# Two layers of routed experts: from whole tiles of one expert to pairs of half tiles, each expert's weights brought from HBM once

## The chip, the cores and the metric

The program runs on one core of a Trainium2 chip (cores 0 to 7; here core 0 alone). The metric is the device time of one execution in microseconds. Runs of this kernel agree within about 0.5%.

## What is computed

The program computes a first transformer block, then two more blocks whose feed-forward part is a mixture of experts. The change touches only these two mixtures. In `second_block`, layer 0 sends 768 tokens (512 and 256 of a context) and layer 1 sends 512 tokens through `hier_moe`:

```python
def hier_moe(h, wg, bg, we, be, w_gate, w_up, w_down):
    g_idx = jnp.argmax(g_logits, axis=-1)                      # 4 groups of 4 experts
    e_sel = jnp.take_along_axis(e_logits, g_idx[:, None, None], axis=1)[:, 0]
    top_p, top_i = lax.top_k(jax.nn.softmax(e_sel, axis=-1), MOE_TOPK)   # 2 experts per token
    ...
    for g in range(MOE_GROUPS):
        a = jnp.einsum('nd,edf->nef', h, w_gate[g])            # 1024 -> 256
        u = jnp.einsum('nd,edf->nef', h, w_up[g])
        hid = jax.nn.silu(a) * u * combine[:, g, :, None]
        out = out + jnp.einsum('nef,efd->nd', hid, w_down[g])  # 256 -> 1024
    return out
```

There are 16 experts of 3 MB each (gate, up and down, 1 MB each, all in float32). Every token goes to two of them, so layer 0 has 1536 rows to compute and layer 1 has 1024. With the given inputs the reference routes this many rows to experts 0 to 15:

```
layer 0: 79 97 97 109 94 105 102 115 86 73 75 72 132 95 107 98
layer 1: 69 77 83 89 37 35 36 36 86 70 62 72 60 77 71 64
```

## The kernel before

The kernel is a list of stages. In a stage the engines work side by side; at its end they all meet (`meet`, L2495). For a mixture the stages are a norm, `Router` (scores, choice of experts, and the normed tokens stored to HBM as `moe_rows`), `Dispatch`, `Experts` and `Combine` (L2428 to L2436).

`Dispatch` (L1710) works out on VectorE where each row goes. Every expert's rows are laid out in tiles of 128 rows, and a tile belongs to one expert. The program can't know how full experts will be, so it always computes the most tiles that could be needed: `tiles_bound` (L1705) gives 27 for layer 0 and 23 for layer 1. With the counts above 17 and 16 of them hold rows; the others are computed all the same, with expert 15. `row_token` says which token stands in which row, `tile_expert` which expert each tile has.

`Experts` (L1844) handles one tile per step, and all its engines run the same software pipeline. In the step of tile t:

- POOL gathers the 128 token rows of a coming tile from HBM (512 KB, L2014).
- TensorE (L1906) multiplies tile t by gate and up (8 products of 128x128 by 128x512, L1917; the profile counts two instructions for each float32 product), transposes the rows of tile t+1 (8, L1889), multiplies tile t-1 by down (4 products, L1902), and transposes the hidden values of tile t (2, L1927).
- ScalarE takes half of each result out of PSUM and issues the DMA that stores a tile's result as `moe_out` (512 KB, L1957). VectorE takes the other half.

Weights come through `ring`, six slots of 1 MB in SBUF shared by all stages. SyncE issues all weight loads in program order (`Ring.fill`, L239). A slot is loaded again when the counter `weights_used` says that TensorE is done with it. For experts `ExpertLoads` (L1796) reads `tile_expert` into a register and loads three slots per tile: two with gate and up for half of the 1024 inputs each (four DMAs of 512 KB in rows of 1 KB, L1830) and one with down (1 MB in rows of 4 KB, L1832). It starts when the lists are ready (L1836). Two tiles' weights fit in the ring. The order of work is given by the program text of each engine and by semaphores; nothing reorders it.

```python
            for c in range(DK):
                g = w.slot(p, c // 4).rearrange("p (c n) -> p c n", c=4)
                last = pe.matmul(ps[:, p, :], mo.xT[:, p, c, :], g[:, c % 4, :], start=(c == 0), stop=(c == DK - 1))
```

## Time and profile before

| | us |
|---|---|
| three runs | 2707.84, 2712.48, 2719.38 (median 2712.48) |
| profiled execution | 2714.23 |
| its span | 2712.4 |
| experts of layer 0, first gather to last down product | about 1571.7 to 1928.0 |
| experts of layer 1, the same | about 2373.7 to 2677.6 |

Times in the trace are counted from the start of the span. "PE" is TensorE, "PEld" its weight loads, "SPq" and "ACTq" the instructions by which SyncE and ScalarE issue DMAs. The DMA share is how much of the time the core's 16 DMA engines had a packet in work. "PEclk" is the granted TensorE clock as a share of 2.4 GHz.

### The profile page before, as it was taken

The numbers are of one execution on the slowest core, as the hardware profiler recorded it, in microseconds if no ns is written. First come the engines' busy times: TensorE is split into PE (matmuls) and PEld (weight loads), VectorE is DVE, ScalarE is ACT, GpSimd is POOL, SyncE is SP. The second block draws the span as 40 slices with busy tenths as digits, with TensorE's granted clock in tenths as the row PEclk, the third lists the DMA queues.
The fourth block names the chain that finished last, engine by engine and source line by source line (L and its number), as shares of the span: only waits on it lengthen the run. The fifth ranks groups of instructions, "written<-read, shape, count | busy, mean of one in ns | idle before, by whom it ended". The sixth has DMA issues, their size and how long they took to land. (4 is left out here: it accounts for less than half of the span.)

```text
span 2712.4 us, 27356 instructions
## 1 busy us (share of the span) xinstructions
PE 2316.3 (85%) x10248; PEld 1270.3 (47%) x10248; DVE 769.3 (28%) x1768; ACT 540.0 (20%) x1153; POOL 151.4 (6%) x159
## 2 busy tenths in 40 slices
PE   5999999899999969997789579999467889579994
PEld 2456554444444435644664534444143665434442
DVE  1012551100010035863532411111237552411112
ACT  1013441100010023221530311111121441211111
POOL 3000000000000001200000000000100000000001
PEclk9997999999999989998999679999788899689997
DMA  7236873112122120010100179999710000199996
GB/s 248 71 93 231 296 282 111 47 62 93 62 86 70 56 97 32 32 62 1 48 17 0 64 261 317 331 334 332 250 65 31 1 1 1 41 307 337 330 335 208
DMA packets 212457, 382.69 MB, mean 141 GB/s; under 512 B 10935, under 2 KB 147351, under 8 KB 206208
## 3 DMA queue, kind: packets, MB, share of 16 engines
q1 hardware_dynamic: 185792, 285.57, 32.5%
q0 software_dynamic: 17312, 62.08, 6.5%
q10 hardware_dynamic: 9248, 33.59, 3.0%
q8 instruction: 73, 1.20, 0.2%
q14 instruction: 32, 0.26, 0.0%
HBM read 344.42 MB, written 42.02 MB: 142 GB/s over the span
## 5 line engine op out<-in xcount | busy, mean ns | idle before, releaser
L1917 PE MATMUL ps<-ring,T 128*128 128x512 f32 x800 | 363.6, 608 | 33.8 <-DMA ring<-in_exp_w_up 25.5
L283 PE MATMUL ps<-ring,HT 128*128 128x512 f32 (+1 forms) x832 | 350.4, 582 | 7.3 <-ACTq L2497 4.3
L2108 PE MATMUL ps<-ring,HT 128*128 128x512 f32 x704 | 304.8, 593 | 3.4 <-issue 2.6
L1917 PEld LDWEIGHTS ps<-ring,T 128*128 128x128 f32 x800 | 150.8, 194 | 217.2 <-issue 217.2
L283 PEld LDWEIGHTS ps<-ring,HT 128*128 128x128 f32 x832 | 158.1, 191 | 197.9 <-issue 188.0
L2108 PEld LDWEIGHTS ps<-ring,HT 128*128 128x128 f32 x704 | 132.9, 190 | 174.7 <-issue 173.7
L1902 PE MATMUL ps<-ring,Z 128*128 128x512 f32 x400 | 180.1, 593 | 1.0 <-ACT Z L1972 1.0
L593 ACT ACTIVATE T<-T,nm 128x128 f32<-128x128 f32 (+5 forms) x208 | 139.8, 673 | 190.8 <-DVE nm L657 190.8
L365 PE MATMUL ps<-ident,T 128*128 128x128 f32 x240 | 39.6, 345 | 141.6 <-DVE T L354 141.6
L547 PE MATMUL ps<-ident,T 128*128 128x128 f32 x752 | 116.4, 288 | 44.4 <-DVE T L315 25.8
L283 PE MATMUL ps<-ring,T 128*128 128x512 f32 x352 | 151.6, 593 | 0.8 <-ACTq L2497 0.7
L1266 PE MATMUL ps<-ring,HT 128*128 128x512 f32 (+1 forms) x384 | 149.2, 545 | 0.5 <-issue 0.5
L2001 DVE TENSOR_TENSOR Z<-ps,Z 128x256 f32<-128x256 f32 x50 | 21.3, 426 | 410.3 <-ACT Z L1965 410.3
L547 PEld LDWEIGHTS ps<-ident,T 128*128 128x128 f32 x752 | 82.0, 143 | 102.3 <-ACT T L593 57.3
L529 PE MATMUL ps<-T 64*128 64x256 f32 (+1 forms) x960 | 118.1, 372 | 10.5 <-DVE nm L657 8.4
L564 PE MATMUL ps<-T,Z 128*64 128x128 f32 x1504 | 111.1, 291 | 0.3 <-DVE T L315 0.3
L1902 PEld LDWEIGHTS ps<-ring,Z 128*128 128x128 f32 x400 | 72.2, 190 | 74.1 <-issue 74.1
L283 PEld LDWEIGHTS ps<-ring,T 128*128 128x128 f32 x352 | 66.7, 190 | 85.1 <-issue 84.2
L365 PEld LDWEIGHTS ps<-ident,T 128*128 128x128 f32 x240 | 38.3, 185 | 145.6 <-issue 145.6
L1266 PEld LDWEIGHTS ps<-ring,HT 128*128 128x128 f32 x384 | 72.0, 191 | 69.4 <-issue 66.0
L2128 DVE TENSOR_TENSOR Z<-ps,T 128x256 f32<-128x256 f32 x44 | 18.7, 425 | 290.1 <-ACT T L2120 290.1
L529 PEld LDWEIGHTS ps<-T 64*128 64x128 f32 x960 | 82.1, 194 | 37.3 <-issue 17.4
(309 smaller groups left out, 2276.0 us busy)
## 6 DMA issues: line engine op xcount, KB each, us to landing
ring<-in_exp_w_gate SPq DMA_DIRECT2D x100, 512.0 KB, 8.0
ring<-in_exp_w_up SPq DMA_DIRECT2D x100, 512.0 KB, 9.1
ring<-in_exp_w_down SPq DMA_DIRECT2D x50, 1024.0 KB, 6.1
ring<-in_mod_w SPq DMA_DIRECT2D x48, 1024.0 KB, 4.8
moe_out<-Z ACTq DMA_DIRECT2D x50, 512.0 KB, 6.6
ring<-in_w_gate SPq DMA_DIRECT2D x22, 512.0 KB, 3.7
ring<-in_w_up SPq DMA_DIRECT2D x22, 512.0 KB, 4.8
ring<-in_w_in SPq DMA_DIRECT2D x10, 1024.0 KB, 15.6
```

Source lines behind the costliest of these rows:

```text
L283: last = pe.matmul(self.banks.bank(u0 + i)[0:self.rows, 0:cn], self.lhs(k0 + c, t), w[:, c, :], start=(k0 + c == 0), stop=(k0 + c == self. ...
L365: last = pe.transpose(self.banks.bank(u)[:, j * P:(j + 1) * P], k.HN[:, t, c * P:(c + 1) * P], k.ident[:, :])
L529: last = pe.matmul(s, u["q"](h), kT(h)[:, done:done + m], start=True, stop=True)
L547: last = pe.transpose(self.t.bank(c)[:, b * P:(b + 1) * P], src, k.ident[:, :])
L564: last = pe.matmul(k.ps[64 * h:64 * h + 64, 7, ui * P:(ui + 1) * P], v(h), self.PT[:, j % 2, h, b * P:(b + 1) * P], start=(b == 0), stop=( ...
L593: act.activation(p, p, ACT.Exp, scale=-1.0, bias=k.nm[:, pi % 2, c:c + 1], accum_out=k.den[:, pi % 2, c:c + 1]).then_inc(k.probs_done.sem, 1)
L1266: last = pe.matmul(self.lin.bank(u)[:, 0:cn], k.HT[:, c, t * P:(t + 1) * P], w[:, c % 4, :], start=(c == 0), stop=(c == DK - 1))
L1902: last = pe.matmul(ps[:, 5 + hf, :], mo.hidT[:, p, c, :], wd[:, c, hf * 512:(hf + 1) * 512], start=(c == 0), stop=(c == 1))
L1917: last = pe.matmul(ps[:, p, :], mo.xT[:, p, c, :], g[:, c % 4, :], start=(c == 0), stop=(c == DK - 1))
L2001: dve.tensor_tensor(mo.hid[:, p, :], ps[:, p, EXH:2 * EXH], mo.silu[:, p, :], ALU.mult).then_inc(self.hid_ready[0], 1)
L2108: last = pe.matmul(self.gu.bank(i), k.HT[:, c, t * P:(t + 1) * P], w[:, c % 4, :], start=(c == 0), stop=(c == DK - 1))
L2128: self.gu.take(i, dve.tensor_tensor(k.Zb(FFN)[:, t, j * EXH:(j + 1) * EXH], self.gu.bank(i)[:, EXH:2 * EXH], k.silub[:, i % 2, :], ALU.mult))
```

## The change

Rows are laid out in half tiles of 64 rows, each of one expert (every expert has at least one). Two neighbouring halves make a pair, which is what a step handles. `pairs_bound` gives 20 pairs for layer 0 and 16 for layer 1. With the counts above, 33 and 25 halves hold rows; the rest, up to 40 and 32, are computed with expert 15.

A product over 128 rows becomes two over 64: the first half's rows go to PSUM partitions 0 to 63, the second half's to 64 to 127, each with its own weights. The expert's weights lie in one of three "places" of 3 MB (the ring's six slots and half of `HT`, now one tensor `wide`). The first half reads its weights from the place. For the second half ScalarE issues two DMAs per pair, which copy the weights within SBUF from the place of that half's expert to fixed buffers: `wgu` (2 MB, gate and up) and `wd` (1 MB, down), two of each.

SyncE now loads each of the 16 experts once per layer, in order, from a new input `experts`, which the host lays out so that each DMA moves 1 MB in rows of 8 KB per partition. Experts 0 and 1 are loaded as soon as the ring's slots are free (before the norm), expert 2 when the router is done with `HT`, and expert e+3 when the last pair of expert e is done (`last_pair`, worked out in `Dispatch`). TensorE and ScalarE read `half_expert` into registers in every step. The loops of `Experts` are written out. The buffers `xg`, `xT` move in SBUF. Only when `Experts` ends may the next stage's weights enter the ring.

```diff
@@ constants
+PLACES = 3
+HALF = 64
@@ Router.tensor
+        pe.drain().then_inc(k.places_free.sem, 1)
@@ bound
-def tiles_bound(tokens):
-    return (2 * tokens - NEXP) // P + NEXP
+def pairs_bound(tokens):
+    return ((2 * tokens - NEXP) // HALF + NEXP + 1) // 2
@@ Dispatch.vector, end
+        do(dve.tensor_scalar(mo.last, mo.end, 0.5, -0.5, ALU.mult, ALU.add))
+        count_of(mo.count, mo.last, NEXP, m - 1, ALU.is_ge)
+        dve.tensor_copy(k.last_pair[:, :], mo.count)
@@ ExpertLoads
...
+        k = self.k
+        sp.wait_ge(k.weights_used, self.n0)
+        for e in range(NEXP):
+            a = e % PLACES
+            if e == PLACES - 1:
+                sp.wait_ge(k.places_free.sem, self.freed + 1)
+            if e == PLACES:
+                sp.wait_ge(k.lists_ready.sem, self.lists + 1)
+            if e >= PLACES:
+                last = sp.value_load(k.last_pair[0:1, e - PLACES:e - PLACES + 1], min_val=0, max_val=63)
+                sp.wait_ge(k.pairs_done.sem, last + (self.done + 1))
+            for j in range(2):
+                sp.dma_start(k.places[:, a, j, :], self.w[e, j]).then_inc(k.gu_landed[a].sem, 16)
+            if e:
+                self.announce_down(sp, e - 1)
+            sp.wait_ge(k.gu_landed[a].sem, self.gu_landed[a] + 32 * (e // PLACES + 1))
+            sp.drain().then_inc(k.experts_ready.sem, 1)
+            if e >= PLACES:
+                sp.wait_ge(k.pairs_done.sem, last + (self.done + 2))
+            sp.dma_start(k.places[:, a, 2, :], self.w[e, 2]).then_inc(k.down_landed[a].sem, 16)
+        self.announce_down(sp, NEXP - 1)
+    def announce_down(self, sp, e):
+        k, a = self.k, e % PLACES
+        sp.wait_ge(k.down_landed[a].sem, self.down_landed[a] + 16 * (e // PLACES + 1))
+        sp.drain().then_inc(k.experts_ready.sem, 1)
+    def expert_of(self, eng, half):
+        return eng.value_load(self.k.half_expert[0:1, half:half + 1], min_val=0, max_val=NEXP - 1)
+    def await_gate_up(self, eng, e):
+        eng.wait_ge(self.k.experts_ready.sem, 2 * e + (self.ready + 1))
+    def await_down(self, eng, e):
+        eng.wait_ge(self.k.experts_ready.sem, 2 * e + (self.ready + 2))
+    def slots(self, e, j0, j1):
+        return self.k.places[:, bass.ds(e % PLACES, 1), j0:j1, :].rearrange("p o j n -> p (o j) n")
+    def columns(self, e, j, c0, n=512):
+        return self.k.places[:, bass.ds(e % PLACES, 1), j, c0:c0 + n].rearrange("p o n -> p (o n)")
@@ Experts.tensor
+        def down(t, e):
+            p = t % 2
+            self.after(pe, self.down_copied[p], 16 * (t // 2 + 1))
             self.after(pe, self.hid_out, t + 1)
-            if not (isinstance(t, int) and t == 0):
+            if t:
                 self.after(pe, self.y_out_act, t)
                 self.after(pe, self.y_out_dve, t)
-            wd = w.slot(p, 2).rearrange("p (c n) -> p c n", c=2)
             for hf in range(2):
                 for c in range(2):
-                    last = pe.matmul(ps[:, 5 + hf, :], mo.hidT[:, p, c, :], wd[:, c, hf * 512:(hf + 1) * 512],
+                    at = 1024 * c + 512 * hf
+                    pe.matmul(ps[low, 5 + hf, :], mo.hidT[:, p, c, low], w.columns(e, 2, at), start=(c == 0), stop=(c == 1))
+                    last = pe.matmul(ps[high, 5 + hf, :], mo.hidT[:, p, c, high], mo.wd[:, p, at:at + 512],
                                      start=(c == 0), stop=(c == 1))
             last.then_inc(self.y_full[0], 1)
-        def step(b, p, final):
-            t = 2 * b + p
-            peeled = isinstance(t, int)
-            w.landed(pe, b, p, 0)
-            w.landed(pe, b, p, 1)
+        x_transposes(0)
+        e = w.expert_of(pe, 0)
+        before = None
+        for t in range(m):
+            p = t % 2
+            self.after(pe, self.gu_copied[p], 16 * (t // 2 + 1))
             self.after(pe, self.x_out_act, t + 1)
             self.after(pe, self.x_out_dve, t + 1)
-            if not (peeled and t < 2):
+            if t >= 2:
                 self.after(pe, self.hid_ready, t - 1)
             for c in range(DK):
-                g = w.slot(p, c // 4).rearrange("p (c n) -> p c n", c=4)
-                last = pe.matmul(ps[:, p, :], mo.xT[:, p, c, :], g[:, c % 4, :], start=(c == 0), stop=(c == DK - 1))
+                j, at = c // 4, 512 * (c % 4)
+                pe.matmul(ps[low, p, :], mo.xT[:, p, c, low], w.columns(e, j, at), start=(c == 0), stop=(c == DK - 1))
+                last = pe.matmul(ps[high, p, :], mo.xT[:, p, c, high], mo.wgu[:, p, j, at:at + 512],
+                                 start=(c == 0), stop=(c == DK - 1))
             last.then_inc(self.gu_full[0], 1)
-            if not final:
-                x_transposes(b + (p == 1), 1 - p)
-            first = peeled and t == 0
-            if not first:
-                down(b - (p == 0), 1 - p)
-            pe.drain().then_inc(k.weights_used, 2 if first else 3)
+            if t + 1 < m:
+                x_transposes(t + 1)
+            if t:
+                down(t - 1, before)
+            pe.drain().then_inc(k.pairs_done.sem, 1)
+            before = e
+            if t + 1 < m:
+                e = w.expert_of(pe, 2 * t + 2)
             self.after(pe, self.hid_ready, t + 1)
             for c in range(2):
                 last = pe.transpose(ps[:, 4 + 3 * p, c * P:(c + 1) * P], mo.hid[:, p, c * P:(c + 1) * P], k.ident[:, :])
             last.then_inc(self.hid_transposed[0], 1)
-        def epilogue(b, p):
-            down(b - (p == 0), 1 - p)
-            pe.drain().then_inc(k.weights_used, 1)
-        self.run(pe, lambda: x_transposes(0, 0), step, epilogue)
+        down(m - 1, before)
+        pe.drain().then_inc(k.pairs_done.sem, 1)
+        pe.drain().then_inc(k.weights_used, SLOTS)
@@ Experts.scalar
+        def gate_up_copy(t):
+            second[t] = w.expert_of(act, 2 * t + 1)
+            if t >= 2:
+                self.after(act, self.gu_full, t - 1)
+            w.await_gate_up(act, second[t])
+            act.dma_start(mo.wgu[:, t % 2, :, :], w.slots(second[t], 0, 2)).then_inc(self.gu_copied[t % 2][0], 16)
+        def down_copy(t):
+            if t >= 2:
+                self.after(act, self.y_full, t - 1)
+            w.await_down(act, second[t])
+            act.dma_start(mo.wd[:, t % 2, :].unsqueeze(1), w.slots(second[t], 2, 3)).then_inc(self.down_copied[t % 2][0], 16)
         def step(b, p, final):
             t = 2 * b + p
             peeled = isinstance(t, int)
+            if not final:
+                gate_up_copy(t + 1)
             self.after(act, self.gu_full, t + 1)
             if not (peeled and t < 2):
                 self.after(act, self.hid_ready, t - 1)
...
             act.activation(mo.hidT[:, p].rearrange("p c n -> p (c n)"), ps[:, 4 + 3 * p, 0:EXH], ACT.Copy).then_inc(self.hid_out[0], 1)
             if not first:
                 y_store(b - (p == 0), 1 - p)
+            down_copy(t)
@@ buffers
+        wide = sb("wide", [P, SLOTS * SLOT + DK * NT * P])
+        k.ring = wide[:, 0:SLOTS * SLOT].rearrange("p (s n) -> p s n", s=SLOTS)
+        k.HT = wide[:, SLOTS * SLOT:SLOTS * SLOT + DK * NT * P].rearrange("p (c n) -> p c n", c=DK)
+        k.places = wide[:, 0:PLACES * 3 * SLOT].rearrange("p (a j n) -> p a j n", a=PLACES, j=3)
+        mo.wd = k.Z[:, at[0]:at[0] + 2 * SLOT].rearrange("p (a n) -> p a n", a=2)
+        mo.wgu = T[:, 0:4 * SLOT].rearrange("p (a j n) -> p a j n", a=2, j=2)
@@ lay_out
+    gate, up = (np.asarray(inputs[n]).reshape(2, NEXP, 2, 4, P, EXH) for n in ("exp_w_gate_2", "exp_w_up_2"))
+    down = np.asarray(inputs["exp_w_down_2"]).reshape(2, NEXP, 1, 2, P, D)
+    both = np.stack([gate, up], 5).transpose(0, 1, 2, 4, 3, 5, 6).reshape(2, NEXP, 2, P, SLOT)
+    a["experts"] = np.ascontiguousarray(np.concatenate([both, down.transpose(0, 1, 2, 4, 3, 5).reshape(2, NEXP, 1, P, SLOT)], 2))
```

The step in the order of the engines. First TensorE, in the middle of a tile's step before (`ps` is PSUM, `Z` and `T` are SBUF buffers):

```order
L1917 MATMUL ps<-ring,T 128x512 x8
L1889 MATMUL ps<-ident,T 128x128 x8
L1902 MATMUL ps<-ring,Z 128x512 x4
L1927 MATMUL ps<-ident,Z 128x128 x2
```

and from the down products of a pair's step to the first gate and up products of the next, now:

```order
L1923 ISA
L1923 MATMUL ps<-wide,Z 64x512
L1924 MATMUL ps<-Z 64x512
L1851 TENSOR_LOAD half_expert
L1851 ISA x2
L1954 MATMUL ps<-ident,Z 128x128 x2
L1940 ISA
L1940 MATMUL ps<-wide,Z 64x512
L1941 MATMUL ps<-T,Z 64x512
```

Each product is now two of half the width, the first with an address worked out in a register (`ISA`); after the down products TensorE's sequencer reads the next pair's expert.

ScalarE, one step before and one now:

```order
L1965 ACTIVATE Z<-ps 128x256 [waits moe_hid_ready,moe_gu_full]
L1945 ACTIVATE T<-ps 128x512 [waits moe_x_transposed]
L1950 ACTIVATE Z<-ps 128x512 [waits y_stored_0,moe_y_full]
L1972 ACTIVATE Z<-ps 128x256 [waits moe_hid_transposed]
L1957 DMA moe_out<-Z 128x1024 [waits moe_y_out_dve,moe_y_out_act]
```

```order
L1992 ISA [waits experts_ready]
L1992 DMA T<-wide 128x4096
L2008 ACTIVATE Z<-ps 128x256 [waits moe_hid_ready,moe_gu_full]
L1970 ACTIVATE Z<-ps 128x512 [waits moe_x_transposed]
L1975 ACTIVATE Z<-ps 128x512 [waits y_stored_1,moe_y_full]
L2015 ACTIVATE Z<-ps 128x256 [waits moe_hid_transposed]
L1982 DMA moe_out<-Z 128x1024 [waits moe_y_out_dve,moe_y_out_act]
L1857 REGISTER_ALU [waits moe_y_full]
L1998 ISA [waits experts_ready]
L1998 DMA Z<-wide 128x2048
```

The copy of gate and up for the next pair stands ahead of the step's first activation, the copy of down for this pair behind its last; both wait for SyncE's word that the expert has landed.

SyncE, the loads at the start of layer 1 and of the first expert that needs a used place, now:

```order
L1835 DMA wide<-in_experts 128x2048 [waits weights_used]
L1835 DMA wide<-in_experts 128x2048
L1842 DMA wide<-in_experts 128x2048 [waits gate_up_landed_0]
L1835 DMA wide<-in_experts 128x2048 x2
L1842 DMA wide<-in_experts 128x2048 [waits down_landed_0,gate_up_landed_1]
L1835 DMA wide<-in_experts 128x2048 [waits places_free]
L1835 DMA wide<-in_experts 128x2048
L1842 DMA wide<-in_experts 128x2048 [waits down_landed_1,gate_up_landed_2]
L1832 TENSOR_LOAD last_pair [waits lists_ready]
```

Three experts' loads now stand ahead of the wait for the lists; all loads stood behind it.

## Rows read from the trace of the kernel before

**Rows 1.** The page: busy time; then busy, clock and DMA tenths in 40 slices.

```profile
PE 2316.3 (85%) x10248; PEld 1270.3 (47%) x10248; DVE 769.3 (28%) x1768; ACT 540.0 (20%) x1153; POOL 151.4 (6%) x159
...
PEclk9997999999999989998999679999788899689997
DMA  7236873112122120010100179999710000199996
```

**Rows 2.** Windows: start:end, length, busy us of engines, PEclk, DMA share, GB/s.

```profile
1494.00:1567.00 73.00, 36.80 (x203) 34.43 (x202) 35.74 (x151) 20.90 (x37) 2.65 (x5) 0.61 0.16 60
1595.00:1919.00 324.00, 304.41 (x865) 141.18 (x866) 44.22 (x75) 46.81 (x101) 22.19 (x24) 0.99 0.99 323
2396.00:2669.00 273.00, 256.31 (x729) 118.86 (x728) 36.30 (x63) 39.17 (x84) 17.92 (x19) 0.99 0.97 321
...
260.00:330.00 70.00, 68.33 (x690) 41.10 (x688) 37.16 (x126) 33.17 (x100) 5.55 (x9) 1.00 0.83 303
```

**Rows 3.** Timeline of TensorE, layer 0: start, length, line, work [idle before <-releaser].

```profile
1583.52 9.87 PE L1917 MATMUL ps<-ring,T 128*128 128x512 f32 x16 [0.94 <-DVE T L1988]
...
1595.15 7.11 PE L1917 MATMUL ps<-ring,T 128*128 128x512 f32 x16 [0.35 <-DVE T L1988]
1602.09 1.04 PE L1889 MATMUL ps<-ident,T 128*128 128x128 f32 x8
1602.97 3.60 PE L1902 MATMUL ps<-ring,Z 128*128 128x512 f32 x8
1606.67 0.43 PE L1927 MATMUL ps<-ident,Z 128*128 128x128 f32 x2
1607.09 7.10 PE L1917 MATMUL ps<-ring,T 128*128 128x512 f32 x16
...
1619.96 0.67 PE L1917 MATMUL ps<-ring,T 128*128 128x512 f32 x1 [0.92 <-issue]
```

**Rows 4.** The page's groups and the waits of 1570 to 1920 us: DMA's part.

```profile
L1917 PE MATMUL ps<-ring,T 128*128 128x512 f32 x800 | 363.6, 608 | 33.8 <-DMA ring<-in_exp_w_up 25.5
...
PE ps L1917 <- DMA ring<-in_exp_w_up: 15.4, 19, 3.0
```

**Rows 5.** DMA queues: packets, MB, share of 16 engines; issues: count, KB each, us to landing.

```profile
DMA packets 212457, 382.69 MB, mean 141 GB/s; under 512 B 10935, under 2 KB 147351, under 8 KB 206208
...
q1 hardware_dynamic: 185792, 285.57, 32.5%
q0 software_dynamic: 17312, 62.08, 6.5%
q10 hardware_dynamic: 9248, 33.59, 3.0%
...
ring<-in_exp_w_down SPq DMA_DIRECT2D x50, 1024.0 KB, 6.1
ring<-in_mod_w SPq DMA_DIRECT2D x48, 1024.0 KB, 4.8
moe_out<-Z ACTq DMA_DIRECT2D x50, 512.0 KB, 6.6
```

**Rows 6.** Timelines: first gather (POOL) and last down products (PE) of both layers.

```profile
1571.71 1.03 POOL L2014 DMA_INDIRECT T<-moe_rows,row_token  x1 [53.84 <-DVEq L2497]
2373.70 0.99 POOL L2014 DMA_INDIRECT T<-moe_rows,row_token  x1 [38.60 <-DVEq L2497]
...
1924.33 3.67 PE L1902 MATMUL ps<-ring,Z 128*128 128x512 f32 x8 [0.52 <-ACT Z L1972]
2673.92 3.67 PE L1902 MATMUL ps<-ring,Z 128*128 128x512 f32 x8 [0.52 <-ACT Z L1972]
```

**Rows 7.** Timelines of TensorE in attention: products onto 64 columns of the array.

```profile
299.31 1.07 PE L558 MATMUL ps<-T,vcmp 31*64 31x512 f32 x4
...
1302.35 1.53 PE L564 MATMUL ps<-T,Z 128*64 128x128 f32 x24
1303.81 0.49 PE L529 MATMUL ps<-T 64*128 64x256 f32 x2
```

**Rows 8.** SyncE's reads of `tile_expert`: ns min/median/max.

```profile
L1820 SPq TENSOR_LOAD <-tile_expert x50: 262/268/485, 1568.1 to 2649.7; - x50
```

**Rows 9.** Timeline of VectorE in `Dispatch`: two of its small steps.

```profile
1556.65 0.21 DVE L1765 TENSOR_SCALAR Z<-Z 128x96 f32<-128x96 f32 x1
1556.90 0.26 DVE L1766 TENSOR_TENSOR Z<-Z 128x96 f32<-128x96 f32 x1
```

More of the change, by code:

```diff
@@ L1767, in vector @@
-        do(dve.tensor_tensor(tile, whole, over_tokens(mo.first), ALU.add))
-        do(dve.tensor_scalar(tmp, whole, -float(P), None, ALU.mult))
-        do(dve.tensor_tensor(rank, rank, tmp, ALU.add))
-        for i in range(2):
-            for x, to in ((tile, mo.at_tile), (rank, mo.at_row)):
-                do(dve.tensor_tensor(tmp, mo.chosen[:, i, 0:n, :], x, ALU.mult))
-                do(dve.tensor_reduce(to[:, i, 0:n], tmp, AXX, ALU.add))
+        do(dve.tensor_scalar(mo.count, mo.count, 1.0 / HALF, None, ALU.mult))
@@ L1835, in fill, with __init__ @@
-    def fill(self, sp):
-        sp.wait_ge(self.k.lists_ready.sem, self.ready + 1)
-        with sp.Fori(0, self.m // 2) as b:
-            self.load(sp, b, 0)
-            self.load(sp, b, 1)
-        if self.m % 2:
-            self.load(sp, self.m // 2, 0)
+    def __init__(self, k, l, A, router, dispatch):
+        self.k, self.w = k, A["experts"][l]
+        self.n0 = k.rg.lend(self)
+        self.freed, self.lists = router.freed, dispatch.ready
+        uses = [len(range(a, NEXP, PLACES)) for a in range(PLACES)]
+        self.gu_landed = [t.reserve(32 * n) for t, n in zip(k.gu_landed, uses)]
+        self.down_landed = [t.reserve(16 * n) for t, n in zip(k.down_landed, uses)]
+        self.ready = k.experts_ready.reserve(2 * NEXP)
+        self.done = k.pairs_done.reserve(dispatch.m + 1)
@@ L1980, in epilogue @@
                 act.wait_ge(self.y_stored[q][0], self.y_stored[q][1] + 16 * ((self.m + 1 - q) // 2))
-        self.run(act, lambda: x_out(0, 0), step, epilogue)
+        self.run(act, first, step, epilogue)
     def vector(self, dve, ch):
```

158 lines of the change are left out of this document (72 added, 86 removed).

## The prediction

> **What bounds the kernel now.** I read the page first, to see where the change can act. TensorE is busy 85% of the span, and the DMA tenths stand at 9 in two stretches only [rows 1]: these are the two `Experts` stages, and they are all that the change is about. The windows over them show DMA shares of 0.99 and 0.97 at 323 and 321 GB/s, and a TensorE clock of 0.99 [rows 2]. So 16 DMA engines have no room left. The timeline of TensorE then shows that it has hardly any either: a step without a wait lasts from 1595.15 to 1607.09, 11.94 us [rows 3], and 27 steps of that are 322 us of the 356.3 us from the first gather (1571.7) to the last down product (1928.0) [rows 6]. The waits agree: TensorE waits for gate and up 15.4 us in layer 0 and 25.5 us in both layers [rows 4]. The two limits are within 6% of each other, so cutting one alone gives little. Layer 1 takes 303.9 us (2373.7 to 2677.6) [rows 6].
>
> **The products.** 50 steps become 36. Each has the same transposes and twice as many products of half the width. Whether that costs a whole step or two is read in attention, where products onto 64 columns of the array alternate between its halves: four instructions of 512 columns take 1.07 us, and 24 of 128 columns 1.53 us [rows 7]. A full-width instruction of 512 costs 0.43 us (8 in 3.60) and one of 128 about 0.11 (8 in 1.04, the last one's tail of 0.16 in it) [rows 3]. One after the other they would take 1.9 and 2.8 us; side by side 1.02 and 1.5. So the halves run side by side, and a pair costs what a tile costs, 11.94 us. Changing between 128 and 64 columns shows no gap at 1303.81 [rows 7]. The new read of `half_expert` stands behind the down products and before the hidden transposes. It costs at least nothing, since the sequencer may be ahead; its load alone is 0.27 us on SyncE [rows 8], and the nearest row for a sequencer that holds up products is the 0.92 us at a loop's start [rows 3]. I take 0.9, as it stands right behind a drain: 12.8 us a step. 36 steps are 461 us; TensorE is then not what ends a stage, if the bytes don't follow.
>
> **The bytes.** They don't. A tile moves 3 MB of weights, 0.5 MB gathered and 0.5 MB stored, 4.19 MB by the issues [rows 5]. A pair moves the same gather and store, 3.15 MB of copies within SBUF, and, while experts are still being loaded, 3.15 MB from HBM per expert: 7.34 MB. The copies run on the same engines and take the place of the loads that were saved. I count what must be moved before the step that first needs expert 15, since after it no load is left. Layer 0, pair 15: gate and up copies of 16 pairs 33.6 MB, down copies of 14 pairs 14.7, 13 stores 6.8, 17 gathers 8.9, and 13 experts without the last down 39.8 (three are there before): 103.8 MB. Layer 1, pair 12 (four pairs there use two experts): 27.3 + 11.5 + 5.2 + 7.3 + 39.8 = 91.1 MB.
>
> The rate has to be chosen. Weights now come in rows of 1 KB; loads become rows of 8 KB, copies at least that. The lower bound is today's mix, 323/0.99 = 326 GB/s [rows 2]. The upper bound is ScalarE's queue with packets of 4 KB: 33.59 MB in 3.0% of 16 x 2712.4 us is 25.8 GB/s an engine, 413 GB/s for 16 [rows 5]. Between them lies the stretch in which `mod_w` is loaded, the only packets of 8 KB or more (6249 of them) [rows 5]: 303 GB/s at a share of 0.83, 365 GB/s at a full one [rows 2]. I take that, since its kind is nearest, and a share of 0.97 as in layer 1 now: 354 GB/s. No row shows a copy within SBUF.
>
> Layer 0: 103.8/0.354 = 293.2 us, then five steps that TensorE bounds, four of 12.8 and one with the last down products (12.8 + 0.5 + 3.7 = 17.0): 361.4 us against 356.3, **+5**. Layer 1: 91.1/0.354 = 257.3, three steps of 12.8 and 17.0: 312.7 against 303.9, **+9**.
>
> The Trainium skill has a rule that weighs these bytes otherwise (SBUF — State Buffer, the summary of rules for kernel authors): reckon 358 GB/s between HBM and SBUF and 436 GB/s within SBUF. By it, as an estimate, the copies (87.1 MB) and the rest (107.8 MB) would take 501 us at a full share and 517 at 0.97, where I have 550.
>
> **Waits that are added.** ScalarE now waits at `gate_up_copy` for the next expert ahead of its silu (L2008), so silu, both PSUM copies, VectorE's product and the down products stand behind a late load. The load of expert e+3 is issued when pair e is done, its copy must follow, and the product is three steps later: 11.3 us of the step, then a load and a copy, each at most one step of 7.34 MB (20.7 us) and about 2 us to land (1 MB of `mod_w` lands in 4.8 us [rows 5], its bytes need 2.9). That is 57 us against three steps of 20.7: covered, by 5 us. SyncE waits for a landing before it issues the next down load; ScalarE's queue has work meanwhile. ScalarE's two further issues and one read a step fall on an engine busy 46.8 of 324 us [rows 2].
>
> **Outside.** Experts 0 and 1 load during a norm and the router, where the DMA share is 0.16 [rows 2]: hidden. Expert 2 starts when the router's last store is still out, and ScalarE waits for that store: between 0 and 2.1 MB/0.354 = 6 us a layer; I take 2, **+4** in all, as the store is half gone by then. `Dispatch` loses 12 of 28 small steps ahead of the one-hots (0.21 to 0.26 us [rows 9], -3) and gains two and longer ones behind them (about +1.5): **-3** for both layers. The next stage's weights start no later than now.
>
> **Sum.** +5 + 9 + 4 - 3 = +15 on the profiled execution's 2714.2: 2729. It stood 1.7 above the median of the three runs, so 2728 against 2712.5. A measurement of this kernel can tell about 0.5% (13.6 us) from no change: this is just outside. With 345 or 385 GB/s in place of 365 the bytes cost 582 or 522 us in place of 550: 2699 to 2760 is this case's own range.
>
> **Rivals.**
> - *Large rows and SBUF copies go faster* (faster than before). At the upper bound of 413 GB/s and 0.97, 194.9 MB take 486 us, 64 less: 2664. It decides from 385 GB/s on. For it: the store's packets do run at that rate. Against: full-share `mod_w` doesn't. By the rule of the Trainium skill above it would be 34 us less, 2694. Chance 0.28.
> - *The rate stays at today's 326 GB/s*, set by three queues in competition: 598 us, +47, 2775. Chance 0.06.
> - *TensorE falls to its low clock.* It would be idle some 8 us of each step of 20.7. The clock was 0.61 in the stretch before the stage [rows 2], and the first gate and up products took 9.87 us, not 7.11 [rows 3]. If only the start of each step runs at 1.2 GHz, that is 2.8 us of idle time. If whole steps do, they last 2 x 11.94 + 0.9 = 24.8 us, over 27 load-bound steps +111: 2839. The Trainium skill (TensorE: Matmul & The Clock Gate, HAM oscillation) says that a wait for DMA in each tile makes every tile start at the low clock; the 9.87 us agree, and it gives the first of these cases. Chance of the second 0.06.
> - *A copy within SBUF costs twice its bytes*, if reading and writing there share something: 87.1 MB more are 246 us, and the last steps become 20.7 too, +59: 3033. No row speaks for or against. Chance 0.06.
> - *The halves don't run side by side*, so the change doesn't do what it says: steps of 23.3 us (24 products of 0.86), 36 of them, ending 218 us later: about 2930. Rows 7 speak against it. Chance 0.04.
>
> The forecast has 0.50. Of it 0.22 lies within 0.5% and 0.01 below, 0.27 above. So faster 0.29, same 0.22, slower 0.49. From 2664 to 2839 the range leaves out about 0.1 above and 0.1 below.
>
> **What would show it.** Right: DMA share 0.95 or more until pair 15 (layer 0) and 12 (layer 1), steps of 19 to 22 us there and near 12.8 in the last four or three; TensorE waiting for DMA `T<-wide`; low clock in single slices. Four instructions of 64x512 in about 1.02 us show the halves. Wrong: GB/s over 385 at a full share, or a share well under 0.95 (then the chain of load, copy and product bounds, not the bytes), or load-bound steps in which TensorE is busy throughout.

## The result and the profile after

| | before | after |
|---|---|---|
| median of the runs, us | 2711.18 | 2808.65 (2803.84 to 2814.07) |
| ratio, 95% interval | | 1.0355 [1.0325, 1.0386] |
| span of the profiled execution | 2712.4 | 2811.8 |
| experts of layer 0, first gather to last down product | 356.3 | 384.1 |
| from there to the first gather of layer 1 | 445.7 | 455.1 |
| experts of layer 1 | 303.9 | 363.5 |

Slower was the likelier sign in the forecast, but it had +0.6% and the chip shows +3.5%. The 99.4 us of span are +27.8 in layer 0, +59.6 in layer 1, +9.4 between them, +1.9 before the first gather and +0.6 after layer 1. The profiled execution of the change is the slowest of its four runs, 5.4 us above their median, and a stretch in which the programs do the same, from the end of `Combine` to layer 1's first gather, takes 396 to 404 us in the profiles of the change and its variants. So a difference of a few us between two stages of two profiles shows little by itself.

The page of the changed kernel, the lines that answer to [rows 1], [rows 4] and [rows 5]:

```profile
PE 2218.0 (79%) x10636; PEld 1168.9 (42%) x10636; DVE 744.4 (26%) x1712; ACT 515.8 (18%) x1097; POOL 138.3 (5%) x145
...
PEclk9997999999999999999997688899698897777787
DMA  7237871112122210001003598897410003777885
...
DMA packets 113437, 424.91 MB, mean 151 GB/s; under 512 B 9175, under 2 KB 43191, under 8 KB 85664
...
q10 hardware_dynamic: 17600, 139.50, 12.5%
...
L1940 PE MATMUL ps<-wide,Z 128*64 x576 | 267.9, 620 | 44.9 <-DMA T<-wide 44.1
L1923 PE MATMUL ps<-wide,Z 128*64 x288 | 180.1, 784 | 132.4 <-DMA Z<-wide 132.4
...
T<-wide ACTq DMA_DIRECT2D x36, 2048.0 KB, 10.8
...
Z<-wide ACTq DMA_DIRECT2D x36, 1024.0 KB, 12.8
```

TensorE now waits 132 us for the copies of the down weights (`Z<-wide`) and 44 us for those of gate and up, where it was idle for 33.8 us in all ahead of the gate and up products [rows 4]. The DMA tenths stood at 9 in both stages; now they stand at 7 to 9 in layer 0 and at 7 to 8 in layer 1: the stages are slower and the DMA engines are not full. The windows, as in [rows 2], for the middle of layer 0 and for two parts of layer 1:

```profile
1616.00:1850.00 234.00, 156.81 (x642) 54.41 (x643) 19.90 (x33) 21.76 (x45) 10.34 (x11) 0.82 0.89 346
...
2497.00:2573.00 76.00, 30.06 (x118) 10.29 (x120) 3.24 (x6) 3.50 (x8) 1.89 (x2) 0.69 0.70 260
2573.00:2727.00 154.00, 101.91 (x404) 34.39 (x400) 12.19 (x21) 12.81 (x27) 6.60 (x7) 0.80 0.88 323
```

The stretch at 2497 holds two steps and lasts 76 us, with a DMA share of 0.70. That is not a bound by bytes. In the middle of layer 0, 346 GB/s at a share of 0.89 would be 389 GB/s at a full one.

The starts of the gate and up products give the steps (the step of a pair lasts until the next pair's products start). Layer 0: 12.2, 19.7, then 20.1 to 22.7 for pairs 2 to 12, then 13.5, 20.0, 13.5 and three of 13.0. Layer 1: 10.7, 17.8, 20.8, 23.8, **38.3, 37.4**, 15.0, **38.9**, 15.3, 22.6, 22.3, 25.5, 15.1, 13.0, 13.2.

One load-bound step of layer 0 on TensorE's timeline, as in [rows 3] (rows that only repeat are left out):

```profile
1701.39 0.64 PE L1940 MATMUL ps<-wide,Z 128*64 x1
1701.39 0.64 PE L1941 MATMUL ps<-T,Z 128*64 128x512 f32 x1
1701.86 0.59 PE L1940 MATMUL ps<-wide,Z 128*64 x1
...
1708.40 1.09 PE L1910 MATMUL ps<-ident,Z 128*128 128x128 f32 x8
1715.22 1.11 PE L1923 MATMUL ps<-wide,Z 128*64 x1 [5.73 <-DMA Z<-wide]
...
1716.13 1.06 PE L1923 MATMUL ps<-wide,Z 128*64 x1
...
1720.69 0.59 PE L1923 MATMUL ps<-wide,Z 128*64 x1
...
1722.09 0.43 PE L1954 MATMUL ps<-ident,Z 128*128 128x128 f32 x2 [0.81 <-issue]
1722.49 0.64 PE L1940 MATMUL ps<-wide,Z 128*64 x1
```

Three things stand here. The two halves' products start within 0.01 us of each other and a pair of them starts every 0.43 us: they run side by side. The read of the register costs 0.81 us. And in the middle of the step TensorE waits 5.73 us for the down copy; the down products behind it take 1.06 us at first, 0.59 at the end. The granted clock is 1.00 from 1701.4 to 1709.4 and 0.50 from 1715.2 to 1719.0: the level of 2.4 GHz, then of 1.2 GHz, then of 2.4 GHz again.

ScalarE's and SyncE's issues around that step say why the copy is late:

```profile
1701.52 0.33 ACTq L1982 DMA_DIRECT2D moe_out<-Z  x1
1702.37 0.49 ACTq L1998 DMA_DIRECT2D Z<-wide  x1
1703.68 0.50 ACTq L1992 DMA_DIRECT2D T<-wide  x1
```

```profile
1700.28 0.34 SPq L1842 DMA_DIRECT2D wide<-in_experts  x1
1701.28 0.81 SPq L1835 DMA_DIRECT2D wide<-in_experts  x2
1721.37 0.34 SPq L1842 DMA_DIRECT2D wide<-in_experts  x1
1722.38 0.81 SPq L1835 DMA_DIRECT2D wide<-in_experts  x2
```

Everything of a step, 3 MB of loads, 3 MB of copies and the store, is issued within 3.5 us (the last 2 MB of copies are the next pair's gate and up). The down copy, the one needed first, competes with 3 MB of loads that TensorE needs much later, and lands 12.8 us after its issue. The step's end is what releases the next bundle.

### The profile page after: what moved, and what is told of

Its sections match the earlier page's. It is cut to its first block and busy times, and to the rows that moved or that the text cites. A ratio compares the mean times of both kernels' runs of the same rounds, so it can differ in the third digit from the quotient of the medians.

```text
span 2811.8 us, 27432 instructions
## 1 busy us (share of the span) xinstructions
PE 2218.0 (79%) x10636; PEld 1168.9 (42%) x10636; DVE 744.4 (26%) x1712; ACT 515.8 (18%) x1097; POOL 138.3 (5%) x145
## 3 DMA queue, kind: packets, MB, share of 16 engines
q1 hardware_dynamic: 80416, 228.93, 23.8%
q10 hardware_dynamic: 17600, 139.50, 12.5%
## 5 line engine op out<-in xcount | busy, mean ns | idle before, releaser
L291 PE MATMUL ps<-wide 128*128 128x512 f32 (+1 forms) x832 | 349.5, 581 | 7.5 <-ACTq L2556 4.3
L2156 PE MATMUL ps<-wide 128*128 128x512 f32 x704 | 304.8, 593 | 3.4 <-issue 2.6
L1940 PE MATMUL ps<-wide,Z 128*64 x576 | 267.9, 620 | 44.9 <-DMA T<-wide 44.1
L1923 PE MATMUL ps<-wide,Z 128*64 x288 | 180.1, 784 | 132.4 <-DMA Z<-wide 132.4
L1941 PE MATMUL ps<-T,Z 128*64 128x512 f32 x576 | 268.0, 620 | 0.0
L291 PEld LDWEIGHTS ps<-wide 128*128 128x128 f32 x832 | 157.7, 191 | 197.4 <-issue 187.5
L2156 PEld LDWEIGHTS ps<-wide 128*128 128x128 f32 x704 | 132.9, 190 | 174.8 <-issue 173.7
L1924 PE MATMUL ps<-Z 128*64 128x512 f32 x288 | 180.2, 784 | 0.0
L1940 PEld LDWEIGHTS ps<-wide,Z 128*64 128x64 f32 x576 | 79.0, 143 | 205.2 <-issue 205.2
L291 PE MATMUL ps<-wide,T 128*128 128x512 f32 x352 | 151.6, 593 | 0.8 <-ACTq L2556 0.7
L1274 PE MATMUL ps<-wide 128*128 128x512 f32 (+1 forms) x384 | 149.2, 545 | 0.5 <-issue 0.5
L1923 PEld LDWEIGHTS ps<-wide,Z 128*64 128x64 f32 x288 | 48.2, 180 | 237.6 <-issue 237.6
L2049 DVE TENSOR_TENSOR Z<-ps,Z 128x256 f32<-128x256 f32 x36 | 15.3, 425 | 433.7 <-ACT Z L2008 433.7
L291 PEld LDWEIGHTS ps<-wide,T 128*128 128x128 f32 x352 | 66.7, 190 | 85.1 <-issue 84.2
L1274 PEld LDWEIGHTS ps<-wide 128*128 128x128 f32 x384 | 72.0, 191 | 69.3 <-issue 66.0
## 6 DMA issues: line engine op xcount, KB each, us to landing
Z<-wide ACTq DMA_DIRECT2D x36, 1024.0 KB, 12.8
wide<-in_w_in SPq DMA_DIRECT2D x10, 1024.0 KB, 14.8
```

The costliest lines, as they stand in the source:

```text
L291: last = pe.matmul(self.banks.bank(u0 + i)[0:self.rows, 0:cn], self.lhs(k0 + c, t), w[:, c, :], start=(k0 + c == 0), stop=(k0 + c == self. ...
L1274: last = pe.matmul(self.lin.bank(u)[:, 0:cn], k.HT[:, c, t * P:(t + 1) * P], w[:, c % 4, :], start=(c == 0), stop=(c == DK - 1))
L1923: pe.matmul(ps[low, 5 + hf, :], mo.hidT[:, p, c, low], w.columns(e, 2, at), start=(c == 0), stop=(c == 1))
L1924: last = pe.matmul(ps[high, 5 + hf, :], mo.hidT[:, p, c, high], mo.wd[:, p, at:at + 512], start=(c == 0), stop=(c == 1))
L1940: pe.matmul(ps[low, p, :], mo.xT[:, p, c, low], w.columns(e, j, at), start=(c == 0), stop=(c == DK - 1))
L1941: last = pe.matmul(ps[high, p, :], mo.xT[:, p, c, high], mo.wgu[:, p, j, at:at + 512], start=(c == 0), stop=(c == DK - 1))
```

## The experiments

Theories ahead of the first four. *Chain*: the down copy's late issue makes each step of TensorE wait and idles the DMA engines in turn. *Bytes*: 7.34 MB a step are the bound and the waits only show it.

**1. The down copy issued early.** The copy of pair t goes to the start of ScalarE's step t, one step's work earlier.

```diff
             if not final:
                 gate_up_copy(t + 1)
+            down_copy(t)
             self.after(act, self.gu_full, t + 1)
...
                 y_store(b - (p == 0), 1 - p)
-            down_copy(t)
```

> The change with the copy of down for pair t issued at the start of ScalarE's step t, right behind the copy of gate and up for pair t+1, and not at its end. Same bytes, same DMAs. Theory 'chain' (a step ends when the late down copy lands, and the down products then run at the low clock): the wait of about 5.7 us ahead of the down products goes, load-bound steps of layer 0 fall from 21.1 us to 19 (7.34 MB at the 389 GB/s that 346 GB/s at a share of 0.89 would be at a full one), the last wait of a stage goes too; the total falls by 35 to 50 us, to about 2765. Theory 'bytes' (346 GB/s is all that the DMA engines give to this mix): steps stay at 21.1 us and the total at 2809, within 6 us.

Measured: 2777.72 us, 1.0251 [1.0234, 1.0269]: 31 us less than the change, where 'chain' expected 35 to 50. Layer 0 takes 365.5 us, layer 1 350.3. The page's two groups of the copies:

```profile
L1940 PE MATMUL ps<-wide,Z 128*64 x576 | 297.0, 675 | 130.6 <-DMA T<-wide 130.4
...
L1923 PE MATMUL ps<-wide,Z 128*64 x288 | 131.2, 598 | 1.2 <-ACT Z L2016 1.2
```

The wait for the down copy is gone, 132 us of it; two thirds come back as a wait for gate and up (130 us where it was 44). In the windows two early steps of layer 0 reach full use of the DMA engines, the rest does not:

```profile
1645.00:1851.00 206.00, 138.29 (x580) 47.63 (x580) 18.09 (x30) 19.64 (x40) 9.40 (x10) 0.83 0.92 352
1611.00:1645.00 34.00, 27.31 (x116) 9.52 (x116) 3.62 (x6) 3.93 (x8) 1.89 (x2) 0.90 0.99 397
```

The steps of pairs 1 to 3 become 14.8 to 18.1 us (19.7 to 21.3 in the change), the later load-bound ones stay at 18 to 23 (19 was expected). So the late copy was real, but something else is behind it. The three long steps of layer 1 don't move: 38.2, 38.6 and 34.1.

**2. The kernel before, with the new layout of weights.** Three DMAs of 1 MB per tile in rows of 8 KB, the rest as before: what large rows are worth alone.

```diff
-            if j < 2:
-                to = slot.rearrange("p (c a n) -> p c a n", c=4, a=2)
-                for i, w in enumerate((gate, up)):
-                    src = w[:, j * 512:(j + 1) * 512, :].rearrange("o (c p) n -> p (o c) n", p=P)
-                    sp.dma_start(to[:, :, i, :], src).then_inc(sem, 16)
...
+            src = self.w[bass.ds(e, 1), j].rearrange("o p n -> p (o n)")
+            sp.dma_start(slot, src).then_inc(sem, 16)
```

> The kernel before with one part of the change alone: expert weights from the new layout, so 3 DMAs of 1 MB in rows of 8 KB per tile in place of 4 of 512 KB in rows of 1 KB and one in rows of 4 KB. If large rows raise the rate (389 GB/s as worked out in the trace of the change), a tile's 4.19 MB need 10.8 us, TensorE's 11.94 us bounds the step, steps fall from 12.76 to about 12.0, and the total by 30 to 38 us, to about 2677. If the rate stays at 326 GB/s, the steps stay and the total is 2711.

Measured: 2705.43 us, 0.9988 [0.9960, 1.0017], no change; 2677 was expected if the rate rose. Four of the six runs took 2701 to 2707 us and two 2725 to 2726; the profile is of one of these two. Its windows over the two stages:

```profile
1595.00:1916.00 321.00, 304.45 (x865) 141.17 (x864) 45.10 (x77) 47.48 (x102) 22.62 (x24) 0.98 0.88 320
2400.00:2660.00 260.00, 242.71 (x682) 112.06 (x682) 35.23 (x61) 38.09 (x82) 18.94 (x20) 0.98 0.87 317
```

Against 0.99 at 323 GB/s [rows 2] the same bytes flow at a share of 0.88, 364 GB/s at a full one, which is the 365 that the forecast took. So the rate rose and the time did not. TensorE is busy 304 of 321 us, so little was left to gain in either case; it still waits 21.1 us for weights in both layers, where it waited 25.5 [rows 4]. Why it waits while the DMA engines have room isn't shown by any run.

**3. The next stage's weights later.** `weights_used` is released one tile before the end of `Combine` instead of at the end of `Experts`.

```diff
@@ Experts.tensor
-        pe.drain().then_inc(k.weights_used, SLOTS)
@@ Combine
+    def tensor(self, pe):
+        pe.wait_ge(self.k.both_done.sem, self.done + len(self.tiles) - 1)
+        pe.drain().then_inc(self.k.weights_used, SLOTS)
```

> The change, but the next stage's weights may enter the ring only when Combine is one tile from its end, not when Experts ends. If Combine's gathers of layer 0 are slowed by those loads (it is the 9.5 us between the end of layer 0's experts and the start of layer 1's that the prediction had at nothing), Combine is as short as before and the total falls by 5 to 9 us, to about 2801. If the loads are needed at once by the next stage, they are late there by as much, and the total stays at 2809 or rises.

Measured: 2801.81 us, 1.0328 [1.0311, 1.0345], 7 us less than the change. The runs of the two overlap (2797 to 2811 us against 2804 to 2814), so the trace has to say where it lies. From the last down product of layer 0 to the end of `Combine` it is 48.6 us in the kernel before, 51.2 in the change and 44.8 here; the other variants of the change took 50.4 to 51.4 without this edit, 44.9 and 44.4 with it (experiments 7 and 8). So the next stage's loads cost `Combine` 6.4 us here, but only 2.6 of them are new: in the kernel before they were issued from 15.6 us before the last down product on. The whole time between the two stages falls from 455.1 to 445.8, that of the kernel before (445.7), but not by this alone: experiment 5, without the edit, has 447.2. Of the change's 9.4 us 2.6 are here and 4.8 less 1.5 in the next mixture's start (see the part on the prediction); the rest is scatter as far as these profiles show. Two of POOL's gathers, with the wait before each, first in the kernel before, then in the changed one:

```profile
1947.67 1.75 POOL L2039 DMA_INDIRECT Z<-moe_out,token_rows  x1 [7.17 <-DVE X L2076]
```

```profile
1980.20 1.95 POOL L2087 DMA_INDIRECT Z<-moe_out,token_rows  x1 [10.46 <-DVE X L2124]
```

**4. Two copies per layer.** Only the first two pairs are copied; from the third on the second half is multiplied with whatever lies in `wgu` and `wd`, so it isn't computed with its own expert's weights. This takes away 64 copies and leaves every product, load, gather and store. TensorE now waits for the loads of the first half's expert alone, so the wait for the second expert of a pair goes too.

```diff
-            if not final:
+            if t + 1 < 2:
                 gate_up_copy(t + 1)
...
-            down_copy(t)
+            if t < 2:
+                down_copy(t)
```

> The change with the copies within SBUF made for the first two pairs of a layer only; later pairs' second halves read what is there (this leaves out 34 of 36 gate and up copies and as many down copies less two, and the second halves' results are not the reference's). TensorE still waits for each expert's loads. Theory 'copies' (bytes and lateness of the copies make the step): layer 0 steps fall to TensorE's 13 us, layer 0's stage from 384 to about 287 us. In layer 1 pairs of two experts still wait for a load that starts only when a place is free, about 12 us more in each of them: from 363 to about 270 us. Total about 2620. Theory 'places' (the reuse of three places holds the steps): layer 0 steps stay at 19 us or more, total 2760 or more.

Measured: 2613.21 us, 0.9638 [0.9619, 0.9658]. Layer 0 takes 286.8 us and its steps 13.1 us from the third on. Without copies the loads and TensorE keep up with each other:

```profile
1636.00:1845.00 209.00, 193.96 (x929) 70.35 (x928) 28.96 (x48) 31.48 (x64) 13.19 (x14) 1.00 0.68 247
```

All that the change costs, and some 98 us that it could have given, hangs on the copies and on what waits for them, the second expert's loads included. Layer 1 takes 262.2 us; two steps of 23.7 and 24.2 remain there, those of pairs 5 and 9, where two pairs in a row use two experts each.

**5 and 6. The long steps of layer 1.** The issues of ScalarE and SyncE in the changed kernel around them:

```profile
2496.06 0.50 ACTq L1998 DMA_DIRECT2D Z<-wide  x1
2526.01 0.50 ACTq L1992 DMA_DIRECT2D T<-wide  x1
2526.62 0.38 ACT L2008 ACTIVATE Z<-ps 128x256 f32<-128x256 f32 x1 [30.77 <-SPq L1839]
```

```profile
2516.11 0.34 SPq L1842 DMA_DIRECT2D wide<-in_experts  x1
2517.13 0.81 SPq L1835 DMA_DIRECT2D wide<-in_experts  x2
2549.02 0.34 SPq L1842 DMA_DIRECT2D wide<-in_experts  x1
2550.03 0.81 SPq L1835 DMA_DIRECT2D wide<-in_experts  x2
```

Pair 4 holds experts 4 and 5, pair 5 holds 6 and 7 (each has at most 64 rows). Expert 7's gate and up are issued at 2517.13, when TensorE's step of pair 4 is done (its own gate and up products ended at 2504.0, but the word to SyncE comes only behind the down products, at 2516.0); they land, ScalarE issues their copy at 2526.01, and pair 5 starts at 2535.2, 38.3 us after pair 4. Expert 8's gate and up could start at the same 2517, since pair 4 was also the last of expert 5, whose place they take. But they stand on SyncE behind expert 7's down load, which waits for the step of pair 5 (2549.02). So load, copy and products come one after the other again, 37.4 us. The third long step, 38.9 us, repeats the pattern: expert 10's place was free at 2549, and its load is issued at 2587.52, right behind expert 9's down load (2586.51). ScalarE's Silu waits 30.8 us behind the copy's wait. There are two candidates: SyncE's queue, and ScalarE's.

SyncE (experiment 5):

```diff
             for j in range(2):
                 sp.dma_start(k.places[:, a, j, :], self.w[e, j]).then_inc(k.gu_landed[a].sem, 16)
-            if e:
-                self.announce_down(sp, e - 1)
+            if e > PLACES:
+                sp.wait_ge(k.pairs_done.sem, before + (self.done + 2))
+            d = e if e < PLACES else e - 1
+            if e != PLACES:
+                self.load_down(sp, d)
+            if e >= PLACES:
+                before = last
             sp.wait_ge(k.gu_landed[a].sem, self.gu_landed[a] + 32 * (e // PLACES + 1))
...
-            if e >= PLACES:
-                sp.wait_ge(k.pairs_done.sem, last + (self.done + 2))
-            sp.dma_start(k.places[:, a, 2, :], self.w[e, 2]).then_inc(k.down_landed[a].sem, 16)
+            if e:
+                self.announce_down(sp, e - 1)
```

> The changed kernel with SyncE's loads in another order: the gate and up load of expert e+1 is issued ahead of the wait for the pair after which the down load of expert e may start. Theory 'queue': in layer 1 a pair of two experts takes two of the three places, and the load of the next expert's gate and up stands on SyncE behind the down load of the expert before it, which waits for that pair's last product; the load is then issued some 20 us earlier, the steps of 37 to 39 us become 22 to 28, layer 1 loses 30 to 45 us and layer 0 (no such steps) less than 5: some 2770 us. Rival 'places': with three places a pair of two experts is served by load, copy and product in series whatever the order of issue, and the time stays within 8 us of 2809. Rival 'bytes': the loads issued earlier only share the DMA engines with the copies, which land later: layer 1 loses under 15 us.

Measured: 2777.31 us, 1.0249 [1.0232, 1.0266]: 31 us less than the change, as 'queue' has it. Layer 1 falls from 363.5 to 330.7, layer 0 by 5.5 to 378.6. The long steps are now 35.3, 24.5 and 28.7. The first stays: it still needs expert 7 loaded and copied after pair 4, as the rival 'places' has it. Expert 8's gate and up are now issued 18 us ahead of expert 7's down load, where they stood behind it:

```profile
2516.19 1.58 SPq L1835 DMA_DIRECT2D wide<-in_experts  x2
2534.03 0.34 SPq L1853 DMA_DIRECT2D wide<-in_experts  x1
2541.57 1.55 SPq L1835 DMA_DIRECT2D wide<-in_experts  x2
```

ScalarE (experiment 6), in layer 1 alone, the copy behind the Silu:

```diff
-            if not final:
+            if not final and self.m == 20:
                 gate_up_copy(t + 1)
...
+            if not final and self.m != 20:
+                gate_up_copy(t + 1)
```

> The changed kernel with one difference, in layer 1 alone: on ScalarE the next pair's gate and up copy, which waits for the load of its expert, is issued behind this pair's Silu and x eviction instead of ahead of them. Theory 'head of line on ScalarE': the long steps of layer 1 come from this wait, behind which the Silu of the present pair stands; they would fall from 38 to under 28 us and the time to some 2770. Theory 'queue on SyncE': TensorE must finish the present pair before the load is issued, the Silu waits for nothing that comes later than the load's own release, and the time stays within 8 us of 2809.

Measured: 2858.07 us, 1.0540 [1.0522, 1.0557]: 49 us **more** than the change, which neither theory had. Layer 1 takes 408.4 us. The long steps stay (32.9, 38.8, 36.7), so ScalarE's wait did not make them. The short ones grew from 11 to 15 us to 20 to 25, because each pair's copy is now issued after the gate and up products of the pair before it, and TensorE waits for it in all 16 steps. The wait of layer 1 is 142.6 us here and 40.4 us in the changed kernel:

```profile
PE ps L1940 <- DMA T<-wide: 142.6, 16, 23.8
```

So the copy stands rightly ahead of the Silu.

**7. The three edits of 1, 3 and 5 together.**

> The changed kernel with the down copy issued at the start of ScalarE's step, SyncE's gate and up load ahead of the wait for the down load, and the next stage's weights loaded one tile before Combine's end. The three gains measured or expected alone are 31, some 35 and 7 us. If they add: 2736 us. If the earlier copy and the earlier load are after the same DMA time in layer 1 (the longest steps were still 38 us with the early copy): some 2745 to 2755. If both together fill the DMA engines to the bound of the bytes (7.34 MB per step at 354 GB/s) no further gain: 2770.

Measured: 2734.87 us, 1.0088 [1.0071, 1.0105]. The gains of 31, 7 and 31 us sum to 69 of the 74 found, so they add, as nearly as these runs can tell. It is still 24 us slower than the kernel before. Layer 0 takes 353.6 us, layer 1 315.8. And now the DMA engines are full, which they were not in the change as made:

```profile
1600.00:1720.00 120.00, 91.42 (x406) 32.30 (x406) 12.63 (x23) 14.30 (x31) 7.41 (x8) 0.90 0.99 382
1720.00:1865.00 145.00, 101.38 (x412) 34.74 (x414) 11.73 (x22) 12.98 (x29) 6.62 (x7) 0.84 0.99 376
2405.00:2640.00 235.00, 151.42 (x638) 52.35 (x634) 18.19 (x33) 19.86 (x44) 10.40 (x11) 0.82 0.94 364
```

Of these versions this is the one whose layer 0 the bytes bound: 7.34 MB at 376 to 382 GB/s are 19.2 to 19.5 us a step. The way from there is fewer bytes, and most copies are of weights that need none.

**8. Copies only for pairs of two experts.** With the given inputs 3 pairs of layer 0 and 4 of layer 1 have two experts. In the other 29 the second half can read the same place as the first, and both halves are one product over 128 rows. TensorE and ScalarE read both experts and branch.

```diff
+            with pe.If(e2 - e == 0):
+                for c in range(DK):
+                    j, at = c // 4, 512 * (c % 4)
+                    last = pe.matmul(ps[:, p, :], mo.xT[:, p, c, :], w.columns(e, j, at), start=(c == 0), stop=(c == DK - 1))
+                last.then_inc(self.gu_full[0], 1)
+            with pe.Else():
...
+            with act.If(alike[t] == 0):
+                w.await_gate_up(act, second[t])
+                act.drain().then_inc(self.gu_copied[t % 2][0], 16)
+            with act.Else():
+                w.await_gate_up(act, second[t])
                 act.dma_start(mo.wgu[:, t % 2, :, :], w.slots(second[t], 0, 2)).then_inc(self.gu_copied[t % 2][0], 16)
```

> The version with all three edits, and with a branch on TensorE and on ScalarE: where both halves of a pair have the same expert, nothing is copied and the 128 rows are multiplied from the place itself in full products; only pairs of two experts are copied and multiplied as halves side by side. Theory 'the copies were the load': with no copy at all behind the second pair the changed kernel took 2613 us; here the pairs of two experts still cost a copy, and their steps stay 20 to 30 us long, of which the layers have some ten together: 2613 + 10 x 3 to 6 us less the 38 us of the three edits in part = 2600 to 2640 us, below the kernel before. Rival 'branches': each step reads two registers more and branches twice on TensorE and ScalarE; if a branch costs 2 us of TensorE's time, 36 steps make 144 us and the version ends at 2730 or above.

Measured: 2640.78 us, 0.9743 [0.9726, 0.9759]: faster than both kernels. Layer 0 takes 300.6 us, layer 1 283.6. A step of TensorE:

```profile
1625.32 7.13 PE L1958 MATMUL ps<-wide,Z 128*128 x16 [0.19 <-issue]
1632.28 1.04 PE L1920 MATMUL ps<-ident,Z 128*128 128x128 f32 x8
1633.16 3.60 PE L1934 MATMUL ps<-wide,Z 128*128 x8
1638.28 0.43 PE L1977 MATMUL ps<-ident,Z 128*128 128x128 f32 x2 [1.52 <-issue]
```

From 1625.32 to 1638.90 it is 13.6 us, where the kernel before took 11.94: 1.52 for two reads behind the drain, 0.19 at the branch. The rival's 2 us per branch don't show. Steps around the pairs of two experts still last 16 to 30 us. The median lies 0.8 us outside the interval that the theory gave (2600 to 2640). The copies left are seven of 2 MB and as many of 1 MB:

```profile
T<-wide ACTq DMA_DIRECT2D x7, 2048.0 KB, 9.1
```

## Why the prediction was right and wrong

Right, by its own steps:

- *Products.* Halves run side by side, and the read costs 0.8 us where 0.9 was taken: steps of 13.0 in the tail against 12.8.
- *The load-bound step of layer 0, by luck.* 20.7 us were forecast and 20.1 to 22.7 came, from two errors that cancel. The full-share rate was taken too low: 365 GB/s, where this mix ran at 389. The share was taken too high: 0.97, where the chain left 0.89. By the prediction's own sums a rate of 385 or more would have made the change faster than before, had the share held; its sign "GB/s over 385 at a full share" came true and was hidden by the chain. With most of the chain cleared (experiment 7) the share is 0.99 at 376 to 382 GB/s, and layer 0 takes 353.6 us and layer 1 315.8 where the forecast's sum had 361.4 and 312.7.
- *Copies don't cost their bytes twice.* ScalarE's queue moved 139.50 MB in 12.5% of 16 x 2811.8 us, 24.8 GB/s an engine or 397 for 16, near the 413 of its stores alone [rows 5].
- *The low clock* came behind waits and not for whole steps: windows of 0.82, single products at 1.06 us. But it came in the middle of a step, in the down products, and not at its start as the rival had it.

Wrong:

- **"That is 57 us against three steps of 20.7: covered, by 5 us."** This step failed most. It holds where each pair uses one expert and three places are three pairs ahead: in layer 0 TensorE waits for gate and up once, 3.7 us. In layer 1 pairs 4, 5, 8 and 9 use two experts, so there the places reach only one or two pairs ahead; and SyncE issues in one order, so a load whose place is free waits behind a down load whose place is not. The steps of 38.3, 37.4 and 38.9 are 52.5 us over three load-bound steps of 20.7; the short ones among them (15.0 and 15.3) give 11 back, so the five steps make some 41 of layer 1's miss of 50.8. The prediction counted the four pairs in its bytes and not in its chain. Experiment 5, with another order alone, is 31 us faster, nearly all of it in layer 1 (33 us between the profiles).
- **The down copy has no term.** The sum of 57 us follows gate and up; the copy of the down weights is counted in the bytes and never put into the chain. It is issued last in ScalarE's step and needed some 7 us later, when the x transposes end, and it lands 12.8 us after its issue beside 3 MB of loads. In layer 0 TensorE waits for it 16 times, 83.2 us in all (5.2 us each), and runs the products behind it at the low clock; the second step is 20 and not 15 us. Layer 0's miss of 22.7 is 16.5 up to pair 15 and 6.2 in the tail (74.4 us where 68.2 were forecast). Experiment 1 puts the late copy at 31 us; between its profile and the change's, which differ by 38, 18.6 us lie in layer 0 and 13.2 in layer 1.
- **"The next stage's weights start no later than now."** They start some 16 us later, when `Experts` ends, and then compete with `Combine`'s gathers: `Combine` is 2.6 us longer (experiment 3).
- **"Between 0 and 2.1 MB/0.354 = 6 us a layer; I take 2, +4 in all."** The wait was seen and taken too small. Expert 2's 2 MB are issued at 1544.24, 0.7 us ahead of the router's last store. The slowest of the router's stores landed 3.6 us after its issue before and 10.2 now (3.0 and 8.7 in layer 1). ScalarE waits for it, and all engines meet behind ScalarE. VectorE's first work in `Dispatch`, before and now in layer 0, and now in layer 1:

```profile
1550.38 0.26 DVE L1743 TENSOR_TENSOR Z<-Z 128x96 f32<-128x96 f32 x1
```

```profile
1555.21 0.26 DVE L1760 TENSOR_TENSOR Z<-Z 128x96 f32<-128x96 f32 x1 [7.04 <-ACTq L2556]
2398.84 0.23 DVE L1760 TENSOR_TENSOR Z<-Z 128x64 f32<-128x64 f32 x1 [4.81 <-ACTq L2556]
```

  That is 11.8 us where 4 were taken. `Dispatch` gave 2.9 and 1.5 back, 4.4 where 3 were taken. No run moves expert 2's load, so its part in the late store is read from the order of issue alone.

So the step that failed is the overlap: the chain of load, copy and product was called covered and is not. The range held because it reached to cases of other causes (rate, clock). The mechanism that decided, a chain across two queues in some pairs, was none of the rivals; the sign that the prediction named for it (a share well under 0.95: then the chain bounds, not the bytes) is what the windows show. The Trainium skill's rule (TensorE: Matmul & The Clock Gate, HAM oscillation), by which a wait for DMA in every tile starts that tile at the low clock, fits the trace with one difference: the down products behind 5.73 us of wait run at 1.06 us, then at 0.59, but the step's gate and up products, 0.8 us behind the work before them, run at the full clock (0.59 us each).

What stays open is how much of experiment 1's gain was the clock and how much the wait itself. By the page's groups the down products are busy 48.9 us less there and the gate and up products 29.1 us more, and the two waits for copies are 45.5 us less together; no run separates them. Nor does a run give SyncE the word that a place is free ahead of the down products, which would be up to 12 us earlier in the step shown.

## What to carry to other kernels

Here the bound by bytes was reached only when the transfers were issued earlier (experiment 7). Before counting on it, a chain of load, copy and product has to be walked for the worst step, not the mean one, and each queue's order of issue checked for a free transfer that stands behind a blocked one. Before weights are copied to give a product its operand, count how often the operand is already in place: here 29 of 36 pairs needed no copy, and a branch and a second register read, under 1 us a step together, avoid them. The transfer that is needed first should be issued first: that alone gave 31 us.

## What was not expected of the hardware

- Larger rows freed DMA engines without moving more: 0.88 share in place of 0.99 at 320 GB/s (experiment 2). The share says how long packets were in work; a share near 1 was no proof that these engines could move no more bytes in larger rows.
- Loads from HBM, copies within SBUF, gathers and stores together ran at 397 GB/s for 34 us (experiment 1) and at 376 to 382 GB/s for 265 us (experiment 7), above the 354 that was forecast for the mix.
- A 1 MB copy within SBUF lands in 12.8 us when it competes with 3 MB of loads, though its bytes need 2.6 us at 397 GB/s. With the early issue of experiment 1 it takes 17.1 us on the page, and nobody waits for it.
- A 512 KB store that was issued 0.7 us behind two loads of 1 MB landed after 10.2 us; without such loads the slowest took 3.6.
- A branch of TensorE to one of two blocks of products costs about 0.2 us, two register reads behind a drain 1.5 us.
